# A decoder in fp32: token-major projections in the first block, seven block products in its down stage

## What is computed

```python
h = rms_norm(x, norm_mix_w)
q_nsa, kv_nsa, g_nsa, q_ret, k_ret, v_ret, g_ret, g_merge = split(h @ w_in)
o_a = nsa_attention(...)                     # [256, 512]
y_a = o_a @ w_nsa_branch                     # 512 x 1024
o_r = head_group_norm(retention(...), ret_gn_w) * silu(g_ret)      # [256, 1024]
y_b = o_r @ w_ret_branch                     # 1024 x 1024
gate_a, gate_b = split(sigmoid(g_merge))     # 2 x [256, 1024]
x = x + (gate_a * y_a + gate_b * y_b) @ w_mix_out
# FFN: up to 2 x 2816, causal convolution of width 3 over tokens
g = up_half * silu(gate_half)                # 256 x 2816
x = x + g @ w_ffn_down                       # 2816 x 1024
```

## Time and profile before

| | us |
|---|---|
| median of 3 runs (1254.57 to 1254.82) | 1254.74 |
| the profiled execution | 1254.49 |
| its span, first to last instruction | 1253.2 |
| PE matmuls busy in the span | 1247.4 |
| DVE | 951.5 |
| ACT | 714.7 |
| POOL | 437.3 |

### The profile page before, as it was taken

One profiled execution on the slowest core, in us unless ns is written; L12 is line 12 of the kernel. 1 busy time (PEld: TensorE's weight loads), 2 busy tenths in 40 slices (PEclk: granted clock), 3 DMA queues, 4 the chain that ended last, 5 costly groups with the idle time before them and its releaser, 6 DMA issues.

```text
span 1253.2 us, 19361 instructions
## 1 busy us (share of the span) xinstructions
PE 1247.4 (100%) x7794; PEld 1120.3 (89%) x7794; DVE 951.5 (76%) x1372; ACT 714.7 (57%) x1026; POOL 437.3 (35%) x346
## 2 busy tenths in 40 slices
PE   9999999999999999999999999999999999999999
PEld 7888899988888889899998888888999998888887
DVE  6865677767887378985767888986898586888895
ACT  7755445377665365575836555545456674655552
POOL 0010011039992069467450112008756743011100
PEclk9999999999999999999999999999999999999999
DMA  7853334545455447644455554555853444545442
GB/s 303 310 211 135 124 129 141 196 185 202 174 197 199 170 168 237 220 164 136 168 191 185 182 200 145 190 210 189 271 188 144 158 168 168 191 181 200 151 166 121
DMA packets 36568, 230.77 MB, mean 184 GB/s; under 512 B 4480, under 2 KB 5120, under 8 KB 10496
## 3 DMA queue, kind: packets, MB, share of 16 engines
q1 hardware_dynamic: 36480, 229.55, 50.9%
HBM read 222.19 MB, written 1.05 MB: 178 GB/s over the span
## 4 chain that ended last, share of the span: by engine, by line
PE 96%; DVE 1%; DMA 1%; ACT 0%; issue 0%; SPq 0%; DVEq 0%
PE ps L608 19%; PE ps L529 10%; PE ps L531 10%; PE ps L530 10%; PE ps L613 10%; PE ps L584 9%; PE ps L585 9%; PE ps L586 9%; PE ps L534 6%; PE ps L548 2%; DMA raw<-in_w 1%; PE ps L677 1%; PE ps L1150 1%; DVE wlo L1955 1%; PE ps L845 0%
## 5 line engine op out<-in xcount | busy, mean ns | idle before, releaser
L1235 ACT ACTIVATE whi<-raw 128x2048 fp32r<-128x2048 f32 (+1 forms) x213 | 401.8, 1891 | 112.6 <-PE ps L531 66.9
L1955 DVE TENSOR_TENSOR wlo<-raw,whi 128x2048 fp32r<-128x2048 f32 (+2 forms) x169 | 383.7, 2276 | 89.0 <-ACT whi L1235 88.0
L1785 POOL TENSOR_TENSOR wlo<-raw,whi 128x512 fp32r<-128x512 f32 x176 | 227.2, 1324 | 90.5 <-ACT whi L1235 87.5
L608 PE MATMUL ps<-hh,whi 128*128 128x512 f32 x1056 | 255.8, 392 | 0.0
L608 PEld LDWEIGHTS ps<-hh,whi 128*128 128x128 f32 x1056 | 193.0, 188 | 36.5
L584 PE MATMUL ps<-hh,whi 128*128 128x256 f32 x640 | 184.1, 288 | 0.0
L586 PE MATMUL ps<-hh,wlo 128*128 128x256 f32 x640 | 181.0, 283 | 0.0
L585 PE MATMUL ps<-hh,whi 128*128 128x256 f32 x640 | 180.9, 283 | 0.0
L1757 POOL TENSOR_TENSOR st<-st,sm 128x1 f32<-128x1 f32 (+2 forms) x28 | 44.8, 1599 | 365.1 <-DVE st L2019 195.1
L613 PEld LDWEIGHTS ps<-hh,wlo 128*128 128x128 f32 x1056 | 137.8, 191 | 6.7
L613 PE MATMUL ps<-hh,wlo 128*128 128x256 f32 x1056 | 139.8, 282 | 0.0
(11 more groups left out here) (350 smaller groups left out, 2266.2 us busy)
## 6 DMA issues: line engine op xcount, KB each, us to landing
raw<-in_w SPq DMA_DIRECT2D x203, 1024.0 KB, 4.8
raw<-in_w SPq DMA_DIRECT2D x8, 256.0 KB, 6.8
kst<-kh SPq DMA_DIRECT2D x16, 128.0 KB, 3.0
qst<-qh SPq DMA_DIRECT2D x16, 128.0 KB, 2.4
raw<-in_w SPq DMA_DIRECT2D x2, 560.0 KB, 12.9
x<-in_x SPq DMA_DIRECT2D x2, 512.0 KB, 5.3
gain<-in_rows SPq DMA_DIRECT2D x2, 512.0 KB, 7.8
kst<-kl SPq DMA_DIRECT2D x8, 128.0 KB, 2.7
```

The source lines that it names most:

```text
L608: pe.op.matmul(o[:, :], wh[:, k, c], t.hh[:, k, :, :], start=k == 0, stop=False, skip_group_check=True)
L1235: act.op.activation(t.whi[i % NHI][:, c], t.raw[i % NRAW][:, c], ACT.Copy).then_inc(*at("act_hi", ("hi", i)))
L1785: pool.op.tensor_tensor(t.wlo[i % NRAW][:, half(k)], t.raw[i % NRAW][:, half(k)], t.whi[i % NHI][:, half(k)].bitcast(F32), ALU.subtract).t ...
L1955: dve.op.tensor_tensor(t.wlo[i % NRAW][:, c], t.raw[i % NRAW][:, c], t.whi[i % NHI][:, c].bitcast(F32), ALU.subtract).then_inc(*at("dve_lo ...
```

## The change

1. **Tokens on the partitions.** gm is four units of 512 and yb two of 512, both through `rows`; ya goes through a new `short_rows` (four k, two token halves). The gates are `gm[n]`, 128 x 2 x 512, scaled per token on the way out of PSUM, token half 0 by DVE (`first_value_out`), half 1 by ACT (`value_out`); `rs0`, `rsT` and `gate_out` go, and with them SP's wait for `rsT` ahead of the loads of `dec` and `ctab`. There are four sigmoids of 1024. The merged data `mg` then have tokens on the partitions and are transposed for mix_out: `mixed_turned`, 16 new transposes, eight within yb1 and twice four within the first half of mix_out; ACT and DVE take the halves out of PSUM (`first_mixed_upper`, `first_mixed_lower`, four each).
2. **Weaving.** How many steps of projections stand behind a step of attention comes from `behind(tt, place)`, and 2, 1, 2, 1 in retention. The rest of the projections runs in a call of its own.
3. **Block sums in `dn0`.** `SEVEN` becomes a tuple for each FFN, with chunks 2, 4 and 6 in the first one. POOL makes `g_sums(0, c)` in its loop behind `glo(5)`, `glo(9)` and `glo(13)`; ACT copies them in its `out(f)` for f - 5 = 4, 8, 12; DVE's `fg` 8, 12 and 16 wait until the sums of their buffer are whole; DVE makes the weight sums and splits of those chunks and, after chunk 6, adds the separate products (`sevens_added`).
4. **POOL splits `dn0`'s second chunk**, between `glo(18)` and `glo(19)`, instead of DVE. ACT splits one chunk further before its last `out`.
5. **Order in `seven`**, in all three FFNs: Q5 (`s5` by `t1`) and the product with `t4` come in front of Q6 and Q7.

```diff
-    for f in range(8):
-        wide(f"gm{f}", "w_in", 0, cols((4376 + 256 * f, 256)), 8, 8)
+    for n in range(4):
+        in1(f"gm{n}", 4376 + 512 * n, 512)
...
-    for f in range(4):
-        wide(f"yb{f}", "w_ret_branch", 0, cols((256 * f, 256)), 8, 8)
+    for f in range(2):
+        wide(f"yb{f}", "w_ret_branch", 0, cols((512 * f, 512)), 8, 4)
...
-    wide("dn0", "w_ffn_down", 0, cols((0, 1024)), NFT, 2)
+    down("dn0", "w_ffn_down", 0)
...
-SEVEN = (1, 3, 5, 7)
+SEVEN = (2, 4, 6), (1, 3, 5, 7), (1, 3, 5, 7)
...
+def behind(tt, place):
+    if place < 3:
+        return (2, (3, 1, 1)[place])[tt]
+    return (2, int(place < 13))[tt]
...
+POOL_LO.add(UNITS["dn0"][1])
...
+    def short_rows(u, hi, lo):
+        i = UNITS[u][0]
+        wh, wl = weights(i, t.whi[i % NHI]), weights(i, t.wlo[i % NRAW])
+        pe.wait_ge(*on("lo", i))
+        for tt in range(2):
+            b = take_bank((u, tt))
+            for k in range(4):
+                mul3(t.pb[b][:, :], hi[:, k, tok(tt)], lo[:, k, tok(tt)], wh[:, k, :], wl[:, k, :], k == 0, k == 3,
+                     [("got", u, tt)] * (k == 3) + [("used", i)] * (tt and k == 3))
...
-    for tt in range(2):
-        pe.wait_ge(*on("rs wide", "n0", tt))
-    b = fixed_bank(("rsT", "n0"), 5)
-    for tt in range(2):
-        ins = pe.op.transpose(t.ps[b][:, tok(tt)], t.xn[0][:, tok(tt)], ident)
-    ins.then_inc(*at("pe_turned", ("rsT", "n0")))
...
+    def mixed_turned(f, tt):
+        turned(("mixT", f, tt), [("merged", "mo", f, tt)], t.mg[0][:, tt, half(f)], 4, 4 + 2 * tt + f)
+
+    for tt in range(2):
+        pe.wait_ge(*on("free", ("oaT", tt, 0)))
+    short_rows("ya0", t.oah, t.oal)
+    for tt in range(2):
+        for g in range(2):
+            turned(("orT", tt, g), [("orr gated", tt)], t.orr[tt][:, half(g)], 4, 4 + 2 * tt + g)
+    short_rows("ya1", t.oah, t.oal)
+    for tt in range(2):
+        for g in range(2):
+            pe.wait_ge(*on("free", ("orT", tt, g)))
+    run(rows("yb0", t.orh, t.orl))
+    g = rows("yb1", t.orh, t.orl)
+    steps(g, 3)
+    for tt in range(2):
+        mixed_turned(0, tt)
+    run(g)
...
-            for k in range(4):
-                part(0, [k], tt)
+        if m:
+            for k in range(4):
+                for tt in range(2):
+                    part(0, [k], tt)
+        else:
+            for tt in range(2):
+                part(0, range(4), tt)
+                mixed_turned(1, tt)
...
+            apart(1, s5, t1)
+            into(banks[1, 0], second(k1), t4, False)
             apart(2, s6, t2)
-            apart(1, s5, t1)
-            apart(3, s7, t3)
-            into(banks[1, 0], second(k1), t4, False, [("used", i + 1)])
+            apart(3, s7, t3, [("used", i + 1)])
...
+        def sums_upper(f):
+            c = f // 2
+            if f % 2 == 0 and c in SEVEN[n]:
+                upper(("g sums hi", n, c), t.gsh[SEVEN[n].index(c)][:, :, :], t.gs[:, :, :], ("g sums", n, c, "whole"))
...
             if f >= 2:
                 g_upper(f - 2)
+            sums_upper(f - 5)
             act.wait_ge(*on("scaled", n, f))
...
-        splits(chunks[0] + AHEAD)
+        splits(chunks[0] + AHEAD + (n == 0))
...
     for f in range(NFT + 6):
         if f in POOL_UP:
             split(*UNITS[f"up0_{f}"])
+        if f == NFT + 3:
+            split(UNITS["dn0"][1])
         if f >= 6:
...
+            if f % 2 and (f - 7) // 2 in SEVEN[0]:
+                g_sums(0, (f - 7) // 2)
...
     def ya_out(f):
...
+        splits(UNITS[f"ya{f}"][0] + AHEAD)
+        dve.wait_ge(*on("gm sigmoid", f))
+        for tt in range(2):
+            name = (f"ya{f}", tt)
             dve.wait_ge(*on("got", *name))
+            dve.op.tensor_tensor(t.mg[0][:, tt, half(f)], bank(name)[:, :], t.gm[f][:, tt, :], ALU.mult).then_inc(
+                *at("dve_out", ("free", name)))
...
             if f >= 4:
                 dve.wait_ge(*on("g", n, f - 4))
-                if n and f % 2 == 0 and f // 2 - 2 in SEVEN:
+                if f % 2 == 0 and f // 2 - 2 in SEVEN[n]:
                     dve.wait_ge(*on("g sums", n, f // 2 - 2, "whole"))
```

More of the change, by code:

```diff
@@ L78, in chunk_plan @@
             wide(f"up{l + 1}_{f}", "w_ffn_in_2", l, cols((128 * f, 128), (FF + 128 * f, 128)), 8, 8)
[L79 to L84, removed]
+        down(f"dn{l + 1}", "w_ffn_out_2", l)
     return plan, units
-SEVEN = (1, 3, 5, 7)
+SEVEN = (2, 4, 6), (1, 3, 5, 7), (1, 3, 5, 7)
 GATES = (8, 9, 10, 11, 0, 1, 2, 3, 4, 5, 6, 7)
@@ L366, in place @@
     t.gs = at("gs", p + 82, [128, 4, 128])
-    t.gsh, t.gsl = ([at(f"{w}{c}", p + o + (4, 8, 40, 30)[c], [128, 4, 128], R32) for c in range(len(SEVEN))]
+    t.gsh, t.gsl = ([at(f"{w}{c}", p + o + (4, 8, 40, 30)[c], [128, 4, 128], R32) for c in range(4)]
                     for w, o in (("gsh", 44), ("gsl", 46)))
@@ L861, in nsa @@
     def nsa():
-        yield
+        yield 2
         n = 0
         for tt in range(2):
-            for m in compressed(tt):
-                yield m
+            for place, _ in enumerate(compressed(tt)):
+                yield behind(tt, place)
                 n += 1
@@ L880, in nsa @@
                     ret_turned("kr", 1)
-    back = chain(*[rows(u, *h) for u in ("vr0", "vr1", "sg0", "sg1")], *[feats(f"gm{f}", *h, 8) for f in range(3)])
-    weave(nsa(), back, 2)
+    back = chain(*[rows(u, *h) for u in ("vr0", "vr1", "sg0", "sg1", *(f"gm{n}" for n in range(4)))])
+    weave(nsa(), back)
     def retention():
@@ L909, in retention @@
                 product(b[:, 256:384], t.krT[:, hd, 128:256], t.qrT[:, hd, 128:256], names=[("ret scores", hd)])
-            yield
+            yield 2
             if hd == 0:
                 heads_turned("oaT", t.oa, 4, lambda tt: ("oa", tt))
[L913 to L927, removed]
+            yield 1
+    weave(retention(), back)
+    run(back)
+    def mixed_turned(f, tt):
[16 more added lines that the diff above has]
+    run(g)
     def part_of(us, hi, lo, data):
@@ L1446, in nsa @@
     def nsa():
-        yield
+        yield 2
         n = 0
         for tt in range(2):
-            for _ in compressed(tt):
-                yield
+            compressed(tt)
+            for place in range(3):
+                yield behind(tt, place)
                 n += 1
@@ L1476, in act_program @@
         rows("sg1", value_out("sg1", lambda tt: t.sg[:, tt, 512:1024], kr_read, first_scale)),
-        *[feats(f"gm{f}", 8) for f in range(2)],
+        *[rows(f"gm{n}", gates_out(n)) for n in range(4)],
     )
-    weave(nsa(), back, 2)
-    splits(UNITS["gm2"][0] + AHEAD)
+    weave(nsa(), back)
     heads_upper("oaT", 4, t.oah)
@@ L1501, in act_program, with first_mixed_upper @@
     gates_sigmoid(1)
-    run(feats("ya0", 4))
+    splits(UNITS["ya0"][0] + AHEAD)
     heads_upper("orT", 8, t.orh)
     gates_sigmoid(2)
-    run(feats("ya1", 4))
+    gates_sigmoid(3)
+    splits(UNITS["ya1"][0] + AHEAD)
+    def first_mixed_upper(f):
+        for tt in range(2):
+            upper(("mixed hi", "mo", f, tt), t.mh[0][:, 4 * f:4 * f + 4, tok(tt)],
+                  bank(("mixT", f, tt))[:, :].rearrange("p (k s) -> p k s", k=4), ("mixT", f, tt))
     def mixed_upper(u, j, m):
         upper(("mixed hi", u, j), t.mh[m][:, j:j + 2, :], t.mg[m][:, j:j + 2, :], ("merged", u, j))
-    for f in range(4):
-        run(feats(f"yb{f}", 8, lambda p: mixed_upper("mo", 2 * f, 0)))
+    run(rows("yb0"))
+    g = rows("yb1")
+    steps(g, 4)
+    first_mixed_upper(0)
+    run(g)
+    first_mixed_upper(1)
     def to_x(u, norm, after):
@@ L1526, in to_x @@
         norm_squares(norm, 1, (), (1,))
-    to_x("mo", "n1", [("free", ("yb3", 0))])
+    to_x("mo", "n1", [("free", ("yb1", tt)) for tt in range(2)])
     fc = small(t, "fconv").rearrange("p (f v c) -> p f v c", f=NFT, v=2)
@@ L1550, in out @@
                 silu(f, "scaled")
-                if f % 2 == 0 and f // 2 - 2 in SEVEN:
-                    c = f // 2 - 2
-                    upper(("g sums hi", n, c), t.gsh[SEVEN.index(c)][:, :, :], t.gs[:, :, :], ("g sums", n, c, "whole"))
+                sums_upper(f - 4)
                 return
@@ L1873, in layer @@
             norm_power(norm_before_ffn, tt)
-        for c in SEVEN:
+        for c in SEVEN[l + 1]:
             g_sums(l + 1, c)
[L1877 to L1898, removed]
     layer(0, "n3", "n4")
```

149 lines of the change are left out of this document (81 added, 68 removed).

## The result

The changed kernel takes 1257.05 us in the median of 21 runs (1255.88 to 1257.89), the kernel before 1254.53 in as many on the same chip: ratio 1.002, 95% interval 1.0015 to 1.0026, so 1.9 to 3.3 us more. The forecast was 1256.2, from 1254.74: 1.4 us more forecast, 2.5 measured. The profiled execution has a span of 1255.2 us against 1253.2, at a mean clock of 0.999.

What follows compares the result with a forecast made beforehand. PE's work was taken to bound the kernel (busy 1247.4 of 1253.2 us). Projections -2.45, dn0 matmuls -2.04 and stalls +5.9 gave +1.4, on the median of 1254.74 so 1256.2 us; range 1250.2 to 1258.6.

Steps and rivals of the forecast that it cites:

- Projections, -2.45: gm, ya, yb: 336 pairs merged at 13.1 ns save 4.4 us; stretches, transposes give some back; net -2.45 us.
- Rival D: Chance 0.03: merging projection matmuls is worth nothing, since merged ones pay the 13.1 ns too; 1260.6 us.
- The matmuls of dn0, -2.04: Down stage: three chunks need 21 matmuls instead of 24, saving 9 x 0.2268 = 2.04 us.
- POOL's lag: First FFN's up stage: block sums make POOL late; glo(13) begins about 369.7 instead of 362.16, sums whole at 372.5.
- ACT's wait: At c=6, ACT stands before its copy of POOL's sums from about 367.8 and waits 4.7 us.
- The stall at the second chunk, 4.0: dn0: POOL's split is ready at 396.4, PE wants it at 392.4, so PE stalls 4.0 us.
- The next stall, 1.5 to 1.7 at the fourth chunk: dn0: DVE's split of the fourth chunk is late, so PE stalls 1.5 to 1.7 us.
- the chain: DVE's queued operations from 396.1, some 12.1 us, end with the fourth chunk's split at 408.1; PE wants it at 406.6.
- Smaller waits, 0.2 to 0.4 at c = 4: dn0: a last PE stall of 0.2 to 0.4 us at c=4.
- B: Chance 0.27: the covers hold, ACT isn't held at c=6 or POOL reaches the second down chunk early enough; 1250.3 us.
- C: Chance 0.15: POOL's lag grows until its last up split is late and PE waits there too; 1258.6 us.

Runs made afterwards that it cites:

- the kernel with both edits: Changed kernel with weight splits of up blocks 13 and 17 on DVE instead of POOL, and POOL's second-chunk split in front of glo(18): 1250.5 us, again 1250.05.
- the sooner split: Changed kernel with POOL's split of dn0's second chunk in front of glo(18) instead of behind it: 1254.14 us, ratio 1.0.

## Why the forecast was right, and where it was not

The forecast of 1256.2 lies 0.85 us below the measured median, and its mechanism is the measured one, with one term missing. Its difference to the kernel before, +1.4, is smaller than the measured +2.5 and than the interval's lower end, 1.9. By its steps:

- **Projections, -2.45.** PE's timeline gives -2.90 at the start of yb (214.08 for 216.98; forecast -3.0 for gm, ya and rsT together); yb takes 22.68 us, 96 x 0.2269 + 0.9, as worked out; mix_out takes 0.96 more (forecast 0.9). Together -2.3; by the run of this half alone -2.2. (The start of yb varies by 1.3 us between profiles, so that agreement within 0.1 is in part luck; and the forecast's terms as printed add up to -2.5, not -2.45.) The rule of the Trainium skill in the page "TensorE: Matmul & The Clock Gate", section "Back-to-back issue gap", by which only 0.8 of the 4.4 gross would be there, would have made this half 1.4 us slower than before instead of 2.2 faster; the run decides against it. Rival D is out.
- **The matmuls of dn0, -2.04.** Exact: 58.51 to 56.47 where nothing waits.
- **POOL's lag.** 7.8 us at `glo(13)`, whole sums within 0.3 us of the time worked out, the split's end within 0.1. Two additions (4.9 and 4.1), less the idle 1.75 each, make 5.5 of it (5.6 measured at the next split, which starts at 348.40); the rest is the DVE split that now falls inside a POOL batch, which is the row at 360.40: 7.28 us for 5.25. ACT's wait was 1.2 us shorter than forecast, since ACT itself was behind by then (its `ghi(15)` at 366.56, 368.9 on the old scale, for 367.46).
- **The stall at the second chunk, 4.0.** Measured 4.0.
- **The next stall, 1.5 to 1.7 at the fourth chunk.** This step failed in form and held in sum. PE waited there for 0.05 us, because 1.7 us of lower clock behind the first stall had taken its place; I had no term for the clock. With the clock kept, the wait appears, 1.6 us. That the missing term cost nothing was luck: 1.7 us of lower clock just filled 1.6 us of wait. The fourth chunk starts at 406.11, 408.4 on the old scale; the chain gave 408.1. Two errors nearly cancel in that: DVE came to its 1536-column split at 392.98, 395.3 on the old scale, for the forecast's 396.1, and took 2.71 us for it instead of 1.76. (The terms of the chain add up to 12.6 us; the 12.1 has the overlaps already off.)
- **Smaller waits, 0.2 to 0.4 at c = 4.** 0.3 there by the distances of the starts, and 0.2 at the fourth chunk.

Sum over dn0: forecast -2.04 + 5.9 = +3.9, measured 62.76 - 58.51 = +4.25. With -2.3 that makes the +2.0 of the spans, against +1.4 forecast. The medians differ by 2.5; the further 0.5 lies outside the span (1.6 us for 1.3 in the profiled executions) and between these and the medians.

Of the rivals, B (1250.3) is what the kernel with both edits gives, 1250.5 and 1250.05: the covers can hold, but not with POOL's load as the change left it. C did not come: POOL's last up split ended at 380.47, 382.8 on the old scale (forecast 382.5), ahead of the 385.0 at which PE wants it.

## What to carry to other kernels

When work goes onto an engine that is off the critical path, count its idle time in the same period as the work, 1.75 us of 22.3 here, and not its busy share over the kernel (35%); what is over adds up period by period. Then follow who waits for it: here POOL's lag reached PE through ACT, whose queue stood for 3.5 us at a small copy, and through DVE, and the cure was to move two unrelated weight splits away, not to touch the place where PE stalled. After a stall is found, ask what would be late next, because filling or removing the first one gives back only what lies between the two (nothing with PE kept busy, 2.6 with the sooner split, of 6.3).

## What the runs showed of the hardware

- A stop of PE of 3.9 us was followed by 3.5 us at the lower clock level (granted clock 0.57 over 394 to 398), 1.7 us lost. With matmuls on zeros in the stop the clock stayed at 1.0. After a stop of 1.77 us, in the kernel where DVE splits the second chunk, it stayed at 1.00 too, and the starts were 0.23 us apart again behind the first. The fall need not come at once: in the kernel with the down stage's changes alone the same stop of 3.9 us, ended at 396.99, was followed by five matmuls at full pace, and only from about 398.6 by some eight that started 0.43 us apart. Its granted clock:

```profile
394.00:398.00 4.00, 1.01 (x4) 0.86 (x5) 3.93 (x3) 2.16 (x2) 2.93 (x2) 1.00 0.00 0
398.00:402.00 4.00, 4.00 (x12) 3.15 (x11) 3.93 (x9) 2.35 (x4) 0.74 (x1) 0.57 0.00 0
```

- When two-input operations of DVE and of POOL alternate, both sides lose. Beside POOL's split of the second chunk the three weight sums and the split behind them took these times (DVE's timeline of the changed kernel), for 1.22, 0.69, 0.69 and 1.76 of the earlier trace rows:

```profile
387.25 2.34 DVE L1984 TENSOR_TENSOR raw<-raw 128x1024 f32<-128x1024 f32 x1
389.63 1.65 DVE L1988 TENSOR_TENSOR raw<-raw,raw 128x512 f32<-128x512 f32 x1
391.31 1.63 DVE L1990 TENSOR_TENSOR raw<-raw,raw 128x512 f32<-128x512 f32 x1
392.98 2.71 DVE L2006 TENSOR_TENSOR wlo<-raw,whi 128x1536 fp32r<-128x1536 f32 x1
```

DVE lost 4.0 us in four operations, POOL 1.6 in its batch (6.85 from 387.22 to 394.07, for 5.25). The forecast had counted 2.2 us for what DVE's operations take from POOL, and 1.76 us for the last DVE split above, as if nothing held it up.
